# A two-block model on one core: the gather work of the expert loop dealt out as single dots and sums, with four gather buffers

## The reference, cut to what matters

```python
def peer(hn, w_q, sub_keys, u_emb, v_emb):
    # each of 512 tokens picks, for 8 heads, 16 of 128*128 experts (128 picks), with softmax gates
    ...
    def chunk(args):
        xc, ec, gc = args
        u = u_emb[ec]
        a = jax.nn.gelu(jnp.einsum('nd,nkd->nk', xc, u))
        return jnp.einsum('nk,nkd->nd', gc * a, v_emb[ec])
...
    h = h + peer(rmsnorm(h, peer_norm_g[l]), peer_w_q[l], peer_sub_keys[l], peer_u[l], peer_v[l])
    return rmsnorm(h, final_norm_g)
```

## Time and profile before

| | |
|---|---|
| median of 3 runs | 4549.65 us (4544.47 to 4549.7) |
| the profiled execution | 4545.25 us, its span 4543.4 us |
| TensorE busy over the span | 4383.8 us (96%), mean granted clock 0.988 |
| VectorE, ScalarE, GpSimd busy | 61%, 38%, 17% |
| expert loop, 3574 to 4530 us of the span | 956 us, TensorE busy 901, VectorE 762, DMA share 0.86, 321 GB/s |
| VectorE waiting there for ScalarE's WH | 160.4 us in 166 waits |
| granted clock 4308 to 4317 us, behind a gap of 2.14 us | 1.00 |
| granted clock 4254 to 4264 us, behind a gap of 3.65 us | 0.68 |

### The profile page before, as it was taken

One profiled execution on the slowest core, in us unless ns is written; L12 is line 12 of the kernel. 1 busy time (PEld: TensorE's weight loads), 2 busy tenths in 40 slices (PEclk: granted clock), 3 DMA queues, 4 the chain that ended last, 5 costly groups with the idle time before them and its releaser, 6 DMA issues. The chain is left out here.

```text
span 4543.4 us, 61954 instructions
## 1 busy us (share of the span) xinstructions
PE 4383.8 (96%) x21945; PEld 3668.2 (81%) x21945; DVE 2753.6 (61%) x4570; ACT 1742.8 (38%) x2923; POOL 755.6 (17%) x783
## 2 busy tenths in 40 slices
PE   8999999999999999999999998899999899999998
PEld 7888888888888887888888886687777788888887
DVE  5436555454344435655454278654778777778787
ACT  3223634332232325344332243442227544444344
POOL 0000000000000000000000000010586543444442
PEclk9999999999999999999999998999999999999999
DMA  3222221222222222311222221031224788888887
GB/s 136 93 102 87 90 84 37 72 96 93 101 93 102 93 92 85 110 47 38 102 93 93 101 95 66 1 139 56 84 93 171 291 324 322 321 319 328 319 332 286
DMA packets 93608, 634.50 MB, mean 140 GB/s; under 512 B 13344, under 2 KB 13728, under 8 KB 22752
## 3 DMA queue, kind: packets, MB, share of 16 engines
q1 hardware_dynamic: 58464, 412.95, 25.0%
q0 software_dynamic: 33792, 193.75, 11.5%
q10 hardware_dynamic: 1152, 25.17, 1.3%
HBM read 604.55 MB, written 27.26 MB: 139 GB/s over the span
## 5 line engine op out<-in xcount | busy, mean ns | idle before, releaser
L193 PE MATMUL PB<-XH,WH 128*128 128x512 f32 (+1 forms) x3288 | 1258.4, 383 | 52.1 <-DVE WL L3312 29.7
L195 PE MATMUL PB<-XH,WL 128*128 128x512 f32 (+1 forms) x3288 | 1236.5, 376 | 0.0
L194 PE MATMUL PB<-XL,WH 128*128 128x512 f32 (+1 forms) x3288 | 1235.7, 376 | 0.0
L174 DVE TENSOR_TENSOR WL<-RAW,WH 128x1024 fp32r<-128x1024 f32 x520 | 624.5, 1242 | 499.8 <-ACT WH L166 459.9
L193 PEld LDWEIGHTS PB<-XH,WH 128*128 128x128 f32 x3288 | 623.0, 189 | 171.3 <-DVE WL L3312 40.9
L194 PEld LDWEIGHTS PB<-XL,WH 128*128 128x128 f32 x3288 | 624.0, 190 | 97.7 <-issue 2.0
L195 PEld LDWEIGHTS PB<-XH,WL 128*128 128x128 f32 x3288 | 621.7, 189 | 100.4
L166 ACT ACTIVATE WH<-RAW 128x1024 fp32r<-128x1024 f32 x504 | 504.5, 1049 | 510.0 <-PE PB L195 481.8
L254 POOL TENSOR_TENSOR SQ<-SQ 128x512 f32<-128x512 f32 x49 | 72.6, 1481 | 2566.3 <-ACT SQ L236 2544.6
L3312 DVE TENSOR_TENSOR WL<-RAW,WH 128x1024 fp32r<-128x1024 f32 x220 | 269.6, 1225 | 163.7 <-ACT WH L3254 162.0
L193 PE MATMUL PB<-WH,WGH 128*128 128x512 f32 x768 | 301.9, 393 | 24.8 <-DVE WGL L3328 24.8
(11 more groups left out here) (441 smaller groups left out, 7087.4 us busy)
## 6 DMA issues: line engine op xcount, KB each, us to landing
RAW<-weights SPq DMA_DIRECT2D x381, 1024.0 KB
gate_matrix<-STG ACTq DMA_DIRECT2D x4, 4096.0 KB, 12.3
GM<-gate_matrix POOLq DMA_DIRECT2D x128, 128.0 KB
RAW<-weights SPq DMA_DIRECT2D x12, 512.0 KB, 3.9
gate_matrix<-STG ACTq DMA_DIRECT2D x3, 2048.0 KB, 7.2
GM<-gate_matrix POOLq DMA_DIRECT2D x128, 48.0 KB
UV<-rows,IDX POOLq DMA_INDIRECT x160
X<-x SPq DMA_DIRECT2D x4, 512.0 KB, 7.7
```

The source lines that it names most:

```text
L174: c.nc.vector.tensor_tensor(c.WL[p][:, cols], c.RAW[p][:, cols], c.WH[p][:, cols].bitcast(F32), ALU.subtract).then_inc(c.sem("w_split"), 1)
L193: c.nc.tensor.matmul(out, wh, xh, start=start, stop=False)
L194: c.nc.tensor.matmul(out, wh, xl, start=False, stop=False)
L195: return c.nc.tensor.matmul(out, wl, xh, start=False, stop=stop)
```

## The change

`round_plan` makes one list of all 160 dots and 160 sums in the order dot 0, dot 1, sum 0, dot 2, sum 1, ..., and deals it to the tiles in shares of 5 for a pair, 3 for a single and 0 for the last tile. A single tile gets two or three of these operations, a pair four or five. The first one of a tile stands where the sum stood before (between `gated` and `gated_low`), the others at the tile's end. Some examples: tile 15 `dot 22 | sum 21`, tile 16 `dot 23 | sum 22, dot 24`, tile 17 (a pair) `sum 23 | dot 25, sum 24, dot 26`, tile 18 `sum 25 | dot 27, sum 26`, tile 52 `dot 76 | sum 75`, tile 106 `dot 155 | sum 154, dot 156`. Before, a tile had the dots of its own steps; now 100 of the 160 dots stand one tile ahead of their step's tile, and dot 156 two. Every dot has a drain in front of it. ScalarE does the gains in each tile by the same plan. `UV` has four buffers instead of three, so a gather waits for sum r-4. `GROW` no longer has a place of its own: it takes two of eight parts of `X`, and its load moves from the head of GpSimd's queue to its end. One semaphore (`kvc_pad`), far ahead of this loop, is removed: ScalarE's wait for a memset of VectorE.

```diff
+UV_SLOTS = 4
...
-            c.UV = [c.sb(f"UV{i}", [P, 2 * D], F32, s) for i in range(3)]
+            c.UV = [c.sb(f"UV{i}", [P, 2 * D], F32, s) for i in range(UV_SLOTS)]
...
-            c.GROW = c.sb("GROW", [P, DC, P], F32, s)
+            c.GROW = c.X[:, 0:2, :].rearrange("p k (h d) -> p (k h) d", d=P)
...
-        act.wait_ge(c.sem("kvc_pad"), 1)
...
+def round_plan():
+
+    ops = [("dot", 0)]
+    for r in range(1, len(ROUNDS)):
+        ops += [("dot", r), ("sum", r - 1)]
+    ops.append(("sum", len(ROUNDS) - 1))
+    room = [0 if x + 1 == len(PLAN) else 5 if len(tile) == 2 else 3 for x, tile in enumerate(PLAN)]
+    at = [len(ops) * sum(room[:x]) // sum(room) for x in range(len(PLAN) + 1)]
+    return [ops[a:b] for a, b in zip(at, at[1:])]
...
-        for n in STEPS_OF[x]:
-            for r in ROUNDS_OF[n]:
+        for what, r in ROUND_PLAN[x]:
+            if what == "dot":
                 pick_gain(r)
...
     def pick_dot(r):
         X = c.XG2 if ROUNDS[r][0] else c.XG
-        dve.wait_ge(c.sem(f"rows_loaded{r % 3}"), r // 3 * 16 + 16)
+        dve.wait_ge(c.sem(f"rows_loaded{r % UV_SLOTS}"), r // UV_SLOTS * 16 + 16)
+        dve.drain()
...
+    def picks(work):
+        for what, r in work:
+            if what == "dot":
+                pick_dot(r)
+            else:
+                if r + 1 == len(ROUNDS):
+                    dve.drain()
+                pick_sum(r)
...
-        rounds = [r for n in STEPS_OF[x] for r in ROUNDS_OF[n]]
+        work = ROUND_PLAN[x]
         if more:
             low(x + 1, 0)
-        else:
-            dve.drain()
-            pick_dot(len(ROUNDS) - 1)
         gated(x, STEPS_OF[x][-1])
         if x:
-            pick_sum(rounds[0] - 1)
+            picks(work[:1])
...
-        if more:
-            pick_dot(rounds[0])
-        for r in rounds[1:]:
-            dve.drain()
-            pick_dot(r)
-            pick_sum(r - 1)
-            dve.drain()
-    dve.drain()
-    pick_sum(len(ROUNDS) - 1)
+        picks(work[1 if x else 0:])
     dve.drain()
...
-    pool.dma_start(c.GROW[:, :, :], gain).then_inc(c.sem("peer_tables_loaded"), 16)
     experts = [e for tile in PLAN for e in tile]
...
-            if r >= 3:
-                pool.wait_ge(c.sem("pick_done"), r - 2)
+            if r >= UV_SLOTS:
+                pool.wait_ge(c.sem("pick_done"), r - UV_SLOTS + 1)
...
+    pool.dma_start(c.GROW[:, :, :], gain).then_inc(c.sem("peer_tables_loaded"), 16)
```

More of the change, by code:

```diff
@@ L2109, in dve_proj2 @@
     V.tensor_copy(c.KVC[:, :, S:S + 32], p2(c, "cmp_pos").rearrange("p (v r) -> p v r", v=2))
-    V.memset(c.KVC[:, :, S + 32:], 0.0).then_inc(c.sem("kvc_pad"), 1)
+    V.memset(c.KVC[:, :, S + 32:], 0.0)
     taps = [(k, tap) for k in (0, 2) for tap in range(CONV_K)]
@@ L3188 @@
 LAST_EXTRA = max(r for r, (x, _) in enumerate(ROUNDS) if x)
+def round_plan():
[6 more added lines that the diff above has]
+    return [ops[a:b] for a, b in zip(at, at[1:])]
+ROUND_PLAN = round_plan()
 def late_before(x):
@@ L3297, in pick_sum @@
         dve.wait_ge(c.sem("pick_gain"), r + 1)
-        V.scalar_tensor_tensor(out=Y[:, :], in0=c.UV[r % 3][:, D:], scalar=c.CF[:, r % 2, 1:2], in1=Y[:, :],
+        V.scalar_tensor_tensor(out=Y[:, :], in0=c.UV[r % UV_SLOTS][:, D:], scalar=c.CF[:, r % 2, 1:2], in1=Y[:, :],
                                op0=ALU.mult, op1=ALU.add).then_inc(c.sem("pick_done"), 1)
@@ L3302, in pick_dot @@
         X = c.XG2 if ROUNDS[r][0] else c.XG
-        dve.wait_ge(c.sem(f"rows_loaded{r % 3}"), r // 3 * 16 + 16)
-        V.scalar_tensor_tensor(out=c.PRODG[:, :], in0=c.UV[r % 3][:, :D], scalar=1.0, in1=X[:, :],
+        dve.wait_ge(c.sem(f"rows_loaded{r % UV_SLOTS}"), r // UV_SLOTS * 16 + 16)
+        dve.drain()
+        V.scalar_tensor_tensor(out=c.PRODG[:, :], in0=c.UV[r % UV_SLOTS][:, :D], scalar=1.0, in1=X[:, :],
                                op0=ALU.mult, op1=ALU.mult, accum_out=c.AV[:, r % 2:r % 2 + 1])\
             .then_inc(c.sem("pick_dot"), 1)
+    def picks(work):
[6 more added lines that the diff above has]
+                pick_sum(r)
     def low(x, half):
@@ L3430, in pool_expert_loads @@
             picks = c.IDX2 if extra else c.IDX
-            if r >= 3:
-                pool.wait_ge(c.sem("pick_done"), r - 2)
-            pool.indirect_dma_start(c.UV[r % 3][:, :], None, rows,
+            if r >= UV_SLOTS:
+                pool.wait_ge(c.sem("pick_done"), r - UV_SLOTS + 1)
+            pool.indirect_dma_start(c.UV[r % UV_SLOTS][:, :], None, rows,
                                     bass.IndirectOffsetOnAxis(ap=picks[:, n:n + 1], axis=0))\
-                .then_inc(c.sem(f"rows_loaded{r % 3}"), 16)
+                .then_inc(c.sem(f"rows_loaded{r % UV_SLOTS}"), 16)
+    pool.dma_start(c.GROW[:, :, :], gain).then_inc(c.sem("peer_tables_loaded"), 16)
 V2 = 3 * LAYERS
```

## The result

| | before | after |
|---|---|---|
| median (lowest to highest) | 4545.36 us (4540.24 to 4549.7), 5 runs | 4572.39 us (4562.01 to 4576.72), 5 runs |
| ratio | | 1.0053, 95% interval 1.0036 to 1.0069 |
| profiled execution, its span | 4545.25, 4543.4 | 4565.19, 4563.4 |

The change makes the kernel about half a per cent slower; 4544 us was predicted, with a range up to 4558. The medians differ by 27.0 us, the spans of the two profiled executions by 20.0, and it is these 20.0 that I account for.

The account below looks back on a forecast made before the run. TensorE's 883.7 us of gap-free products plus gaps bound the loop; the excess went from 68.4 to 68.2 us, which with start (-0.8) and tail (-0.3) made -1.3 on 4545.25: 4544 us. Range 4528 to 4558.

Parts of the forecast that it names:

- the 883.7 of gap-free products: TensorE's products in the expert loop without any gap: 883.7 us, against 952.1 before, so 68.4 us were to be had.
- VectorE's waits for rows over 30 us: Sign of being wrong: VectorE's UV waits over 30 us, where 10 to 20 in tiles 52 to 109 were expected.
- Pairs by the tail rule: At the 17 new pair tiles: TensorE's gaps, set by which operations end tiles, sum to 52.3 us, 3.1 per pair.
- Four buffers, next limit `wg_ready`: On GpSimd: `wg_ready` is what is late next, with the gather 2.66 us after `gated` of two steps before.
- I take 6.1+0.6 = 6.7: A gather's rows land 6.7 us behind its issue (bounds 5.5 and 8.2); early dots then cost TensorE 7.3 us.
- Dot 156: In tile 106, two tiles ahead: waits 3.8 us for rows, 4.2 at TensorE, and 1.5 of slow clock.
- Slow clock: TensorE's lower clock after long gaps: its 10.4 us go, since no part of a gap exceeds 2.5 us.
- Start: Ahead of product 0: moving `GROW`'s load gains 0.6 to 2.0 us, tile 0's two dots cost 0.5; net gain 0.8.
- GROW at the end, the tail: At the kernel's end: `GROW`'s load is hidden (bare, up to 7 us); the tail gets 0.3 us shorter.
- Rows late: Rival, slower: rows landing from 7.5 us on delay dots in a tile's middle, +15 to +25, 4562 us; chance 0.13.
- Weights late: Rival, slower: RAW lands a microsecond late at each of 17 pairs, +10 to +17, 4557 us; chance 0.1.
- Rows in time: Rival, faster: rows land 5.5 to 6 us behind the issue, early dots wait for nothing, 4534 to 4530 us; chance 0.27.

Follow-up runs that it names:

- e1: The kernel after with each step's gathers put ahead of the `wg_ready` wait and GM loads in GpSimd's queue; 4536.24 us, 0.9969 of before.
- e3: The kernel before with four UV buffers, `GROW` in `X` and loaded last, and `kvc_pad` removed; the old deal kept; 4529.9 us, 0.9956 of before.
- e7: e2_no_dot_ahead with three UV buffers instead of four; 4664.46 us, 1.0254 of before.
- e4: The kernel after with three UV buffers instead of four; 4637.95 us, 1.0192 of before.
- e9: e6_lagged_deal with each step's gathers issued one step later, behind the next step's gate loads; 4535.68 us, 0.9977 of before.
- e6_lagged_deal: The kernel after with each tile's share moved back four operations, then clipped so no dot is ahead of its step; 4629.95 us, 1.018 of before.
- e10_gathers_first_no_dot_ahead: e2_no_dot_ahead with the gathers issued first, as in e1; 4614.9 us, 1.0146 of before.
- e5_dot_then_sum: e1 with a closing sum and dot swapped to dot and then sum, `AV` and `CF` four deep; 4508.46 us, 0.9914 of before.
- e8_whole_rounds_by_room: The kernel after with another `round_plan`: whole rounds (dot r, sum r-1) dealt by room, fewer just ahead of pairs, none ahead of its step; 4492.8 us, 0.9876 of before.
- e2_no_dot_ahead: The kernel after with the deal clipped so no dot stands ahead of its own step's tile; 4513.86 us, 0.9925 of before.

## Why the prediction was wrong, point by point

The frame held. From product 0 to the end of the last product the kernel before takes 952.5 us (3580.85 to 4532.99 + 0.39), the one after 975.9 (3577.47 to 4552.95 + 0.39); over the 883.7 of gap-free products that is 68.8 and 92.2, where 68.2 was predicted for after. (The prediction's 68.4 for before holds two small slips: the last row has two followers, not six, so the products end at 4533.38; and its three terms as written add up to 883.5.) Of the 92.2, 67.8 stand in 39 gaps (48.7 for WGL, 19.1 for WL) plus 0.17 each, 74.4 in all, against 64.3 predicted (52.3 + 7.3 + 4.2 + 0.5); the other 17.8 are slow clock and rest, against 3.9. Of the prediction's own signs of being wrong, one came: VectorE's waits for rows over 30 us.

- *Pairs by the tail rule: right in sum.* To 4010 there is almost no waiting for rows (5.0 us in 6), so the rule stands alone there: the first eight pairs have 22.0 us of gaps (20.0 in 12 rows and 0.17 each), the rule gives 24.7; single pairs are up to 1.3 us off either way. In e1, where early dots hardly wait, it can be held against all 17 pairs: 34 gaps of 43.5 us, 49.3 with 0.17 each, where the rule gives 52.3. In the trace after, a dot that ends a tile at 3782.82 has the next `low` at 3785.64, 2.82 behind it (the rule: 2.81).
- *Four buffers, next limit `wg_ready`: right.* Gather 2.65 us behind `gated` as in the earlier trace rows, GpSimd's wait moved to WG.
- *"I take 6.1+0.6 = 6.7": this is the step that failed.* The median landing is 8.4. The reading was right for the kernel before (its median is 6.15), and carrying it over to four buffers was the mistake. Before, GpSimd waited 447 us for sums, so most gathers were issued when a sum had ended; I read a duration under one discipline of the queue and used it under another (the last section has the landing of each kernel beside that wait). With it the wait of an early dot in a tile's middle came out at 0.8 to 2.6 us; the 12 that waited did so for 3.1 on average, up to 5.0. Dot 156 itself waited only 0.4 where 3.8 was predicted, since dot 155 ahead of it had waited 3.3. Taking the rule's share for the other nine pairs (27.6), the start's 2.4 and the first eight's 22.0 from 74.4 leaves 22.4 us of TensorE's gaps for early dots and dot 156, where I had 11.5. The working had a bound for it ("about 12 places x 1.5 more and four gaps over 3 us, 25 more"), 4569 us, and the profiled execution is at 4565.19; the range left that bound out.
- *Slow clock: wrong, for two reasons.* "No part exceeds 2.5" was true of nearly all of the tail rule's gaps alone. A late row added to one of them made 4.61, 4.28, 4.49 and 3.85 us (4023.39, 4234.61, 4291.79, 4398.81) and 3.32 at the last tiles, and the windows of 10 us from 4023, 4234, 4291, 4398 and 4537 have a clock of 0.83. A landing off by 1.7 us thus cost twice. The second reason is the premise that "gaps of 2.1 to 2.3 left the clock at full". It held in the kernel before, but in the one after the clock also fell to 0.83 behind gaps of 2.06 (3660.47), 2.64, 2.03, 2.44 and 2.32 us, and in e3 behind five of eight gaps of 1.98 to 2.33. And it stayed at 1.00 from 3577 to 3587, behind product 0's gap of 3.33. The length of the gap alone does not tell. So part of the slow clock would have stayed without a late row.
- *Start: not borne out.* The wait ahead of product 0 fell from 4.68 to 3.33 us, and 1.35 is within the 0.6 to 2.0 given for GROW, and the 1.7 of slow clock that the sum kept there are gone; but tile 0's second dot costs 2.19 + 0.17 at 3584.00, where 0.5 was taken. That product 0 starts 3.4 us earlier says little: in the eight executions of kernels with the changed code ahead of the loop and GM(0) at the head of GpSimd's queue it starts anywhere from 3574.56 (e7) to 3585.66 (e4). *GROW at the end, the tail:* from the last product to the end of the span 10.06 us against 10.02, nothing.
- *Rivals.* "Rows late" described what happened, in place and in price (+15 to +25, from a landing of 7.5 on), and had 0.13; against it stood only the mean of seen landings, which was no evidence for four buffers. That the range ended at 4558 was thus a judgement, not bad luck. "Weights late" did not happen (3.3 us in 2 waits). "Rows in time" was the wrong side of the same number.

The Trainium skill (DMA: Bandwidth & Descriptors, Anatomy of one DMA) gives 4.4 us for such a gather, an estimate from its fit; no run agrees: the medians are 6.15 us before and 6.4 to 8.4 in the others, and the longest in the kernel after is 14.3. Its table of latencies in the same page (Latency and other measured facts) says that HBM's latency rises under load, which goes the same way; no run here separates that from queueing.

Left open: what makes the landing longer. A longer issue on GpSimd (median 1.54 us against 1.03 before) does not decide it: e3 has the short issue (1.04) and lands in 8.1, e7 the long one (1.71) and lands in 6.4. No run held the number in flight fixed while changing the load.

## What to carry to other kernels

A duration of a transfer belongs to the waits under which it was issued: when a change adds a buffer, take its landing from the longest that the trace shows or beyond, not from the mean of those that were waited for. In an in-order DMA queue that serves two consumers, each plan of the consumers has its own right order: before moving work, write down for every load what it waits for and what stands behind it, since the same swap gained 0.8% on one plan and lost 2.2% on another. And place optional work so that the engine owes nothing when the dense stretch begins (a round less ahead of each pair), rather than evenly.

## What the runs showed of the hardware that I had not expected

The time from a gather's issue to its landing goes with how freely GpSimd may issue. The table has, for each kernel, GpSimd's wait for sums from 3580 to 4530 and the median landing. In the kernel before and in e9 some landing events are missing; their medians are of the 129 and 128 gathers that can be matched.

| kernel | buffers | waits for sums, us | median landing, us |
|---|---|---|---|
| e6_lagged_deal | 4 | 560.8 | 6.6 |
| e7_no_dot_ahead_3_slots | 3 | 544.5 | 6.4 |
| e10_gathers_first_no_dot_ahead | 4 | 513.0 | 6.6 |
| before | 3 | 447.2 | 6.15 |
| e5_dot_then_sum | 4 | 442.6 | 6.8 |
| e1_gathers_first | 4 | 423.7 | 7.3 |
| e4_deal_alone | 3 | 421.8 | 6.9 |
| e8_whole_rounds_by_room | 4 | 332.3 | 7.6 |
| e2_no_dot_ahead | 4 | 309.1 | 7.7 |
| e9_lagged_gathers_later | 4 | 255.7 | 8.0 |
| e3_slots_alone | 4 | 114.0 | 8.1 |
| after | 4 | 68.8 | 8.4 |

It does not go with the count of buffers as such: e6 and e10, with four, land nearly as e7 does with three. That the freedom is the cause is not shown. Whether more transfers in flight or the gate loads issued right ahead of each gather make it longer, these runs don't tell apart. The issue alone takes GpSimd 0.97 us at best, with medians of 1.00 in e5, 1.54 after and 1.71 in e2 and e8. The core moved 338 GB/s over 916 us at a DMA share of 0.91 with hardly a wait for weights, where 321 at 0.86 had looked near full.
